# Tokens gathered as high and low halves, for two expert groups at a time, in a two-block transformer kernel on one Trainium2 core

## The reference

```python
# 16 experts in 4 groups of 4; a token takes the best group and two experts in it
g_sel = argmax(group_score); eid = the two best experts in group g_sel
gate[t, e] = normalised weight of the two, 0 elsewhere
for e in range(16):                       # layers 0, 1
    h = silu(xt @ w_gate[e]) * (xt @ w_up[e])       # 1024 -> 512
    y = y + gate[:, e:e+1] * (h @ w_down[e])        # 512 -> 1024
# layers e, o: the same with sigmoid affinities, on
h = rmsnorm(x, norm_ffn) * (1.0 + scale_f) + shift_f      # scale_f, shift_f: one row of 1024
x = x + gate_f * moe(h)
```

## Time and profile before

| | us |
|---|---|
| median of 3 runs | 2360.33 (2354.33 to 2363.47) |
| the profiled execution | 2360.78 |
| its span, first to last instruction | 2358.8 |
| expert stage of layer 0 / 1 / e (with the overflow's start) / o, by windows | 309 / 311 / 326 / 329 |
| engines busy: PE, DVE, ACT, POOL | 2140.4, 1593.5, 1150.1, 60.3 |

### The profile page before, as it was taken

The page is one execution under the profiler, slowest core; times in us unless marked ns, Lnnn a source line. Parts: engine busy times, 40 slices in busy tenths (PEclk is TensorE's granted clock), DMA queues, the critical chain, the costliest instruction groups (busy, mean ns, idle before and its releaser), DMA issues.

```text
span 2358.8 us, 25347 instructions
## 1 busy us (share of the span) xinstructions
PE 2140.4 (91%) x9668; PEld 1656.1 (70%) x9668; DVE 1593.5 (68%) x2031; ACT 1150.1 (49%) x1246; POOL 60.3 (3%) x86
## 2 busy tenths in 40 slices
PE   8999899999799988999969887999989687899996
PEld 4657578888556657888858756778877474787785
DVE  2744579888464457888853556778868654688786
ACT  1202167767020115777723444777667332577773
POOL 0100000000000000000000000000000000000000
PEclk9999899999899988999989897999999899899999
DMA  9765289999675617999945113889989221698893
GB/s 406 304 231 214 89 303 344 351 339 346 243 285 216 265 54 285 334 349 344 343 167 211 36 37 141 325 315 333 343 310 349 95 108 43 220 337 328 313 339 124
DMA packets 53901, 596.65 MB, mean 253 GB/s; under 512 B 5777, under 2 KB 7825, under 8 KB 15505
## 3 DMA queue, kind: packets, MB, share of 16 engines
q1 hardware_dynamic: 34560, 500.19, 56.6%
q0 software_dynamic: 8352, 59.77, 6.3%
q10 hardware_dynamic: 10864, 35.00, 4.1%
HBM read 591.79 MB, written 3.15 MB: 252 GB/s over the span
## 4 chain that ended last, share of the span: by engine, by line
PE 67%; issue 17%; DVE 7%; ACT 4%; DMA 4%; ACTq 0%; POOL 0%; DVEq 0%; POOLq 0%
PE bank L694 63%; PE bank L724 2%; DMA hi_ring<-in_ada 1%; PE bank L963 1%; DMA x<-in_x_in 1%; DMA hi_ring<-in_weights 1%; DVE work L1665 1%; DVE ring_parts L1665 1%; ACT mix L1267 1%; ACT hi_ring_parts L1267 1%; DVE mix L1791 1%; ACT work L1267 1%; DVE hi_ring L2075 0%; ACT xT L1267 0%; ACT oT_parts L1267 0%
## 5 line engine op out<-in xcount | busy, mean ns | idle before, releaser
L1665 DVE TENSOR_TENSOR ring_parts<-ring,hi_ring_parts 128x2048 fp32r<-128x2048 f32 x398 | 893.5, 2284 | 190.3 <-ACT hi_ring_parts L1267 189.9
L1267 ACT ACTIVATE hi_ring_parts<-ring 128x2048 fp32r<-128x2048 f32 x398 | 747.1, 1910 | 131.6 <-PE bank L694 98.0
L694 PE MATMUL bank<-hi_ring_parts,oT_parts 128*128 128x512 f32 (+1 forms) x1088 | 356.0, 390 | 9.3 <-DVE ring_parts L1665 8.7
L694 PE MATMUL bank<-hi_ring_parts,xT_parts 128*128 128x512 f32 x1024 | 336.4, 396 | 17.7 <-DVE ring_parts L1665 14.1
L694 PE MATMUL bank<-hi_ring_parts,work_parts 128*128 128x512 f32 x1024 | 326.2, 390 | 5.7 <-DVE work_parts L1665 5.7
L1267 ACT ACTIVATE work<-bank 128x512 f32<-128x512 f32 (+6 forms) x211 | 110.6, 527 | 439.6 <-PE bank L694 426.1
L694 PEld LDWEIGHTS bank<-hi_ring_parts,oT_parts 128*128 128x128 f32 x1088 | 204.5, 188 | 53.5 <-issue 14.0
L694 PEld LDWEIGHTS bank<-hi_ring_parts,xT_parts 128*128 128x128 f32 x1024 | 192.3, 188 | 64.3 <-issue 22.1
L694 PEld LDWEIGHTS bank<-hi_ring_parts,work_parts 128*128 128x128 f32 x1024 | 192.2, 188 | 46.6 <-DVE work_parts L1665 6.6
L694 PE MATMUL bank<-ring_parts,oT_parts 128*128 128x512 f32 (+1 forms) x576 | 219.2, 381 | 0.0
L694 PE MATMUL bank<-ring_parts,xT_parts 128*128 128x512 f32 x512 | 199.5, 390 | 0.0
(11 more groups left out here) (222 smaller groups left out, 2436.1 us busy)
## 6 DMA issues: line engine op xcount, KB each, us to landing
ring<-in_weights SPq DMA_DIRECT2D x238, 2048.0 KB, 7.9
hi_ring<-in_ada POOLq DMA_DIRECT2D x48, 1024.0 KB, 10.9
hi_ring<-in_weights ACTq DMA_DIRECT2D x48, 512.0 KB, 6.1
work<-in_vecs POOLq DMA_DIRECT2D x8, 1024.0 KB, 5.0
bias_rows<-work ACTq DMA_DIRECT2D x8, 256.0 KB, 5.4
work<-bias_rows ACTq DMA_DIRECT2D x2, 1024.0 KB, 7.7
params<-in_prm ACTq DMA_DIRECT2D x1, 1389.5 KB, 13.1
consts<-in_cst ACTq DMA_DIRECT2D x1, 1040.0 KB, 18.8
```

The costliest lines, as they stand in the source:

```text
L694: ins = nc.tensor.matmul(o, lhsT, rhs, start=start, stop=stop)
L1267: return nc.scalar.activation(o, i, f, **kw)
L1665: return v.tensor_tensor(o, a, b, op)
```

## The change

1. `src_hi` and `src_lo`: the 256 token rows are split once a layer into a rounded part (ACT, `src_high`) in `work` at 0, and a low part (DVE, `src_low`) over `x` (layers 0, 1) or `mix` (e, o). In layers 0 and 1 ACT writes ALPHA x into `mix` first (`scaled`), which DVE did before.
2. Groups are gathered in pairs: `pick` for two groups is 128 x 256 for each T, once as fp32r for the gather and once as fp32 for `at` and `sg`. A gather is eight products (four of the high part, four of the low), each of four matmuls of 256 columns. ACT copies the high results, DVE the low ones, straight from PSUM to the tokens' homes. The first pair is gathered before expert 0, the second in the places of up 4 and up 5. A third home is added.
3. The overflow's gather is made inside its branch only.
4. In the last expert of each group up k+1 comes before down k, in PE's order, in the order of the pieces, and in ACT's and DVE's lists. DVE's `scattered` comes behind the split of up k+1, not before it.
5. Layers e and o: `mix` is now modulated on DVE (two products with a row of gains, one sum with a row of shifts, a tile T), and the turned rows are only copied. The two rows are made by PE (`modulation_rows`) and copied by ACT.
6. Since `work` at 0 is now used in each layer, `memT` is loaded again for layer 1 and the bias again for layer o. The scratch of POOL's transfers goes from 8192 to 4096 bytes. In the router DVE writes the slots from the rank in one step (two instructions where there were five; two come later, in `beyond`).

```diff
+                def chosen(q, low):
+                    src = src_lo(tag) if low else src_hi
+                    return [(c * 2 * P, (c + 1) * 2 * P, P,
+                             [(src[:, T, (2 * q + c) * P:(2 * q + c + 1) * P], pick_parts[:, T, :]) for T in range(NT)])
+                            for c in range(2)]
+                def gather(j, half):
+                    pe.wait_ge(pick_ready, 2 * SET_BASE[tag[0]] + 4 * j + 2)
+                    for q, low, name in gather_names(tag, j, half):
+                        product(name, chosen(q, low))
+                def places(j):
+                    pe.wait_ge(pick_ready, 2 * SET_BASE[tag[0]] + 4 * j + 4)
+                    transposes(f"{tag}.at{j}", [((NT * s + T) * P, (NT * s + T + 1) * P, P, pick[:, T, s, :])
+                                                for s in range(2) for T in range(NT)])
+                    product(f"{tag}.sg{j}", [(PER_GROUP * s, PER_GROUP * (s + 1), P,
+                                              [(pick[:, T, s, :], r_a[:, T, :]) for T in range(NT)]) for s in range(2)])
                 release[0] += owed[0] - 1
-                gather_a(0)
-                gather_b(0)
+                gather(0, 0)
+                gather(0, 1)
+                places(0)
...
                 for k in range(NEXP):
-                    g, e = divmod(k, PER_GROUP)
-                    if k < NEXP - 1:
+                    last = k == NEXP - 1
+                    if not last:
                         gate(k + 1, 0)
-                        turn_hidden(k)
+                    turn_hidden(k)
+                    if not last:
                         gate(k + 1, 1)
-                    else:
-                        gather_b(GROUPS)
-                        turn_hidden(k)
+                    if not last and up_first(k + 1):
+                        up(k + 1)
                     down(k)
-                    if e == 0:
-                        gather_a(g + 1)
-                    if e == 1 and g < GROUPS - 1:
-                        gather_b(g + 1)
-                    if k < NEXP - 1:
-                        gate_up("u", k + 1)
-                    if e == PER_GROUP - 1:
-                        scatter(g)
+                    if not last and not up_first(k + 1):
+                        up(k + 1)
+                    if k % per == per - 1:
+                        scatter(k // per)
```

In the branch, PE's list (DVE makes the picks before it, ACT and DVE copy between; four transposes of `pick` and the sums of the gates are left out):

```diff
+                    pe.wait_ge(ov_picked, 2 * NT * (layer + 1))
+                    for q in range(DC // 2):
+                        for low in range(2):
+                            whole_bank(2 * q + low, chosen(q, low))
+                    pe.wait_ge(ov_tok_hi, DC // 2 * (layer + 1))
+                    pe.wait_ge(ov_tok_lo, DC // 2 * (layer + 1))
...
+                    pe.wait_ge(ov_placed, 2 * (layer + 1))
                     wide("g", 0, range(4))
```

DVE's loop in `experts`, and the rows of layers e and o:

```diff
+                split("u", 0)
                 for k in range(NEXP):
-                    g, e = divmod(k, PER_GROUP)
-                    split("u", k)
-                    if e == 0 and g:
-                        y_lo(g - 1)
-                    if k < NEXP - 1:
+                    last = k == NEXP - 1
+                    if k % per == 0 and k:
+                        y_lo(k // per - 1)
+                    tokens_low(k)
+                    if not last:
                         split("g", k + 1)
...
                     h(k)
+                    if not last and gather_at(tag, k + 1) and gather_at(tag, k + 1)[1] == 0:
+                        picks(2 * gather_at(tag, k + 1)[0], pick_ready)
+                    follows = k % per == 0 and k
+                    if not last and up_first(k + 1):
+                        split("u", k + 1)
+                    split("d", k, (0,))
                     hidden(k)
                     split("d", k, (1,))
-                    if e == 0 and g:
-                        scattered(g - 1)
-                    if e == 2 and g < GROUPS - 1:
-                        low_tokens(g + 1)
+                    if not last and not up_first(k + 1):
+                        split("u", k + 1)
+                    if follows and per == PER_GROUP:
+                        scattered(k // per - 1)
...
                     rstd(1)
-                    tell_row(v.tensor_scalar(mix[:, T, :], x[:, T, :], stat_out[:, T:T + 1], None, ALU.mult))
+                    for q in range(2):
+                        c = slice(q * 512, (q + 1) * 512)
+                        (step if q else step.later)(v.scalar_tensor_tensor(
+                            out=mix[:, T, c], in0=x[:, T, c], scalar=stat_out[:, T:T + 1], in1=mod_rows[:, 0, c],
+                            op0=ALU.mult, op1=ALU.mult))
+                    tell_row(tt(mix[:, T, :], mix[:, T, :], mod_rows[:, 1, :], ALU.add))
```

ACT, ahead of layer e's first turned rows and at the start of the expert stages:

```diff
+            def turned_and_split(tag, turn, n):
+                src_high(tag, 0, NT * n + 1)
+                turned(turn)
+                src_high(tag, 1, NT * n + 2)
+                if tag[0] in "01":
+                    scaled(tag)
...
             for T in range(NT):
                 act.dma_start(bias[:, :, T, :], skewed(255 - P * T)).then_inc(bias_back, 16)
+            modulation_rows("e")
             modulated("e.turn0", 0, 0, True)
```

More of the change, by code:

```diff
@@ L57 @@
 PER_GROUP = NEXP // GROUPS
-GATHERS = GROUPS + 1
 N_CMP = (S - 32) // 16 + 1
@@ L965, in wide @@
                     def wide(what, e, parts):
-                        o = psum[e % 2 if what == "g" else 2 + e % 2][:, :]
+                        o = psum[e % 2 if what == "g" else OV_UP][:, :]
+                        b = 2 * (e // per)
                         for q, w in zip(parts, quarters(tag, what, e, parts)):
@@ new lines, in modulation_rows, with experts, high, places @@
+            def modulation_rows(tag):
+                for k, name in enumerate(("scale", "shift")):
+                    for q in range(2):
+                        whole(mod_rows[:, k, q * 512:(q + 1) * 512], f"{tag}.{name}.{q}")
+            def experts(tag):
+                layer, per = MOE_LAYER[tag[0]], PER_SET[tag[0]]
+                sets = SETS[tag[0]]
+                def high(j, half):
+                    for q, low, name in gather_names(tag, j, half):
+                        if not low:
+                            carry(name, [(token_pair(j, q, 0), lambda t: t[:, :].rearrange("p (c s n) -> p c s n", c=2, s=2))])
+                def places(j):
+                    carry(f"{tag}.at{j}", [(place_pair(j), lambda t: t[:, :].rearrange("p (s n) -> p s n", s=2))])
+                    carry(f"{tag}.sg{j}", [(slot_gate[:, 0:2 + j % 2:1 + j % 2, :],
+                                            lambda t: t[:, 0:2 * PER_GROUP].rearrange("p (s n) -> p s n", s=2))])
+                high(0, 0)
+                high(0, 1)
+                places(0)
+                def split(what, k, halves=(0, 1)):
+                    split_expert(tag, PLACE_OF[what, k], halves)
@@ L2009, in experts @@
                     hidden(k)
                     split("d", k, (1,))
-                    if e == 0 and g:
-                        scattered(g - 1)
-                    if e == 2 and g < GROUPS - 1:
-                        low_tokens(g + 1)
-                low_tokens(GROUPS)
-                y_lo(GROUPS - 1)
-                scattered(GROUPS - 1)
-                for T, n, name in scatter_names(tag, GROUPS - 1):
+                    if not last and not up_first(k + 1):
+                        split("u", k + 1)
@@ L2019, in experts @@
+                    if follows and per == PER_GROUP:
+                        scattered(k // per - 1)
+                y_lo(sets - 1)
+                scattered(sets - 1)
+                for T, n, name in scatter_names(tag, sets - 1):
                     banks.wait_drained(dve, name)
                 for n in range(2):
-                    banks.wait_drained(dve, f"{tag}.{GROUPS - 1}.{n}.y")
+                    banks.wait_drained(dve, f"{tag}.{sets - 1}.{n}.y")
                 over = dve.value_load(control[0:1, 4 * layer:4 * layer + 1], min_val=0, max_val=GROUPS)
@@ L2028, in low @@
                             tt(w.lo, w.raw, w.hi, ALU.subtract).then_inc(ov_lo, 1)
-                    low("g", 0)
+                    picks(sets, ov_picked)
+                    for q in range(DC // 2):
+                        dve.wait_ge(ov_gathered, (DC + 2) * layer + 2 * q + 2)
+                        v.tensor_copy(token_pair(1, q, 1), psum[2 * q + 1][:, :].rearrange("p (c s n) -> p c s n", c=2, s=2)) \
+                            .then_inc(ov_tok_lo, 1)
+                    low_of("g", 0)
@@ L2100, in adaptive_norm @@
                 rstd(2)
-                gained(layer, gain, scale)
+                step(gained(layer, gain, scale))
                 for T in range(NT):
@@ L2121, in take_gate, with gated_rows @@
                     drained(f"{tag}.{q}", v.tensor_copy(gate_row[:, q * 512:(q + 1) * 512], p_[:, :]))
-            def gated_rows(tag, turn, layer, gain, scale, shift):
```

(1 more changed line is left out.)

475 lines of the change are left out of this document (291 added, 184 removed).

## The result

| | before | after |
|---|---|---|
| median of four runs | 2360.44 us | 2302.28 us |
| lowest to highest | 2354.33 to 2363.47 | 2299.91 to 2304.83 |
| the profiled execution, its span | 2360.78, 2358.8 | 2304.83, 2302.9 |

The ratio is 0.9757 (95% interval 0.9733 to 0.9781): 58 us faster. The forecast was 2312, its range 2296 to 2336. Between the profiled executions the span falls by 55.9 us, against 49.2 forecast.

The account below looks back on a forecast made before the run. PE's own list was taken as the bound in layer 0, with waits on top in layer e. Loops -63.4, heads +1.1, start of e +1.3 and overflow +11.8 gave -49.2 us: forecast 2312 us, range 2296 to 2336.

Parts of the forecast that it names:

- What bounds the kernel: Expert stages: PE's own list bounds layer 0 (busy 73.8 of 74 us a group); layer e adds some 3 us of waits.
- Gathers removed, and stalls that go: Loop: four gathers costing PE 16.6 us a layer go, with stalls of 1.9 (layers 0, 1) or 12.8 (e, o).
- The pair: One paired gather added in each layer's loop, 32 matmuls of 256 columns and 12 small ones: 4.9 us.
- The stall that comes: PE waits for DVE's later sums: 0.75 us at k = 8 and 12, about 1.7 at k = 4; 3.2 a layer.
- The order of up and down: Up ahead of down at group ends: priced at nothing; without cover, about 1 us at four places a layer.
- Loads: Weight pieces of the ring, each now serving 5.6 us instead of 6.2: no cost, with 4.7 us of cover.
- rival C: Ring loads pace the kernel, making it slower than before; deciding point 6.34 us a piece, 2387 us at 6.5; chance 0.05.
- Heads and the start of e: Work ahead of expert 0: heads +1.1 us over the layers (ends -3 and +6); start of layer e +1.3.
- Overflow: Layer e's branch: a gather chain now precedes PE's first product, +11.8 us, ends 6 and 16.
- B: DVE becomes the bound once PE is lighter, at 64.4 of 69 us a group: 2349 us; chance 0.12.
- D: The change does not do what it says (second layer enters the branch, or more fp32r passes): about 2330 us; chance 0.02.
- A: The new stalls in the loops do not come and the overflow's chain is short: 2293 us; chance 0.17.

Follow-up runs that it names:

- e1_sum_between: Changed kernel with DVE's four sums over a group's scatter placed between the two halves of the split of up k+1; 2291.0 us, ratio 0.9715.
- e1_sum_first: Changed kernel with DVE's four sums over a group's scatter put back in front of the split of up k+1; 2295.5 us, ratio 0.9726.
- e3_picks_early: Changed kernel with DVE's sums between split halves, the overflow's first two weight quarters split earlier, and its picks moved out of the branch; 2290.6 us.
- e3_before_scratch4k: The kernel before the change, with only its DMA scratch cut from 8192 to 4096 bytes; 2360.4 us, ratio 0.9996.

## Why the prediction was right, and where it was off

- **What bounds the kernel.** Right, and the runs show it twice: PE is busy for 69.03 of 69.03 us in a group once DVE's sums are out of its way, and taking a third of its list away gives 89 us.
- **Gathers removed, and stalls that go.** 18.5 us forecast a layer in 0 and 1, 29.4 in e and o. From the loops, with the pair (5.2) and the new stalls (2.4 to 2.5) put back, it was 19.8 and 30.3. A group before was 74.1 us and is 69.0 without pair and stalls, so a gather with its small stalls was 5.1 us, not 3.6 + 0.6 + 0.5 = 4.7.
- **The pair.** 4.9 forecast; the two intervals that hold it in `e1_sum_between` are 5.2 us longer than the same intervals without a gather, 16.8 and 18.6 us (16 matmuls from first to last take 1.79 us, 0.12 apart, as read from the earlier trace rows).
- **The stall that comes.** Named at the right places, with the right releaser and size: 0.71 us at up 9 and up 13 (forecast 0.75), 1.0 at the middle gather (forecast 1.7). The term was 2.4 to 2.5 us, not 3.2.
- **The order of up and down.** The prediction said that down 14 covers hidden row 15: shown, 1.1 us. What it did not see is the rest of that cover's worth, 2.3 us a layer of waits and slow clock behind the turn. Its price without the cover, about 1 us at four places a layer, is near the measured 3.4 us a layer by luck: the steady groups do not change, so three of the four places cost nothing, and the fourth costs three times its price.
- **Loads.** Right that they cost nothing, but not for the reason given. The prediction counted 4.7 us of cover for each load. ACT, which had hardly waited for the ring before (0.5 to 2.5 us a loop), waits 12.3 to 24.2 us a loop for it, up to 2.8 us at a time, so at those loads no cover is left. PE does not notice: in `e1_sum_between` ACT waits 7.8 us in the steady group in which PE has no idle time. It is ACT's slack that pays for them. The prediction's sign of rival C was there, at a harmless size.
- **Heads and the start of e.** The terms that the prediction writes out (+0.9; -1 + 1.9 - 1.2 in e and in o) make +0.3, not the +1.1 of its sum. In the first three such rows of the table +2.2 forecast, +2.9 measured, with the parts off by 1.5 to 2.3 us each way. In the eleven kernels with this head the router of layer 0 starts between 281.4 and 285.8, so one trace does not tell such terms from scatter.
- **Overflow.** +11.8 forecast, +8.9 measured to the first product: the gather's 32 matmuls took 5.4 us and not 6.8 (half of them at 1.2 GHz, behind 3.8 us of idle time of PE; the prediction priced all of them at half clock), and DVE began the picks 3.5 us behind its first sum and not 4.4. The rest of the row is +1.2 from there to o's router and -1.3 in o's head.
- **The tail.** Forecast 0, measured +1.9: 1.6 of it is PE's last row product, 3.58 us in place of 2.02, at a granted clock of 0.64 and not 1.00. In `e1_sum_first`, whose tail is the same code, it took 2.05 and the tail 31.4 us, so the clock decides; but four other kernels with this tail have 33.0 to 33.2. Ahead of that product PE is idle for 3.36 us and not 3.11. The longer wait does not settle the clock: in `e3_picks_early` the wait is 2.90 us and the product takes 3.78, in `e1_sum_first` 3.37 and 2.05, and `e3_before_scratch4k`, with the old code, has 4.35 and 3.50. Why it is slow in one execution and not in another stays open.
- **Rivals.** B (DVE the bound, 2349) is refuted for this kernel, but its arithmetic was good: it put DVE's list at 64.4 us a group, and 65.0 is where the group lands when PE leaves the way, though ACT waits for loads there as well. C's point of decision, 6.34 us a piece, is far off: the ring gives a piece each 5.1 us (61.35/12). C's own figures do not close either: no row gives its 6.02 us a piece (the loops' 192 pieces took 6.1 us each before and take 5.8 now), and from 6.02 and 2312 a pace of 6.5 would make 2404 us, not 2387. D did not happen. A (stalls do not come and the overflow's chain is short, 2293) did not happen either; `e1_sum_between` has A's loops, not its branch, at 2291.

The gain was 6.7 us larger than the sum: 6.2 from the loops (1.25 to 1.8 a layer), 3.2 from the overflow's row, 2.6 back in heads and tail. The largest terms were read from rows of the same operation and came within 10%, which is why the result lies inside the range; that the smaller misses partly cancel is luck.

## What to carry over

When one engine's own list is the bound, a moved instruction of another engine costs exactly what the bound engine then waits for: follow the banks and the halves by name, and put the mover between the two halves of the work it would delay. Where an engine waits for a short step, the price is the wait and then the clock: two waits of 0.9 and 2.1 us cost 1.4 to 1.8 more. A chain in a branch that runs once is worth ordering too, but shortening one link shows the next (a load that lands 4.4 us after its issue), so look at all of them first.

## What was not expected of the hardware

- Matmuls of constants in an otherwise idle wait bring the next gather to a higher granted clock: 1.00 with 12 of them and 0.72 with 7, against 0.64 without (3.91 and 5.11 us against 5.68, layer 0). The 7, which end before the data come, gain 5 us over four places (21.3 to 22.4 us from router to expert 0 against 23.0 to 23.1); the 12, which end too late, 1.5.
- Two short idle times of PE 0.66 us apart (0.91 and 2.14 us) were followed by 3.5 us at 0.52; a single one of 1.41 us at the same place was not. Whether the 2.14 us alone would do it no run shows.
- How many matmuls of the same branch run at the slow clock differs between kernels whose branch is the same (8, 15, 23, 25), which moves the time by up to 3.4 us. Edits of that size are read from the trace's stretches, not from a median.
- The ring gives 361 GB/s at a DMA share of 0.95 when PE takes a piece each 5.8 us, and 394 to 400 at 0.97 to 0.98 when it is asked for more: the share near 1 did not mean that the ring was at its end.
